# The delta-rule scan of a hybrid diffusion step: level products over all 128 rows of the TensorE array

## The reference

```
def step(S, inp):
    r_t, w_t, k_t, v_t, kk_t, a_t = inp
    sa = einsum('bdhvk,bdhk->bdhv', S, -kk_t)
    S = S * w_t[..., None, :] + sa[..., None] * (kk_t * a_t)[..., None, :] + v_t[..., None] * k_t[..., None, :]
    return S, einsum('bdhvk,bdhk->bdhv', S, r_t)
```

## Time and profile before

| what | value |
|---|---|
| median of 3 runs (lowest to highest) | 4503.6 us (4500.49 to 4511.37) |
| the profiled execution, its own time | 4488.36 us |
| its span | 4486.5 us |
| TensorE products busy, share of the span | 4088.9 us, 91% |
| VectorE busy | 2644.1 us, 59% |
| ScalarE busy | 1940.2 us, 43% |
| granted TensorE clock, mean over the span | 0.966 of full speed |

### The profile page before, as it was taken

How to read it: one execution, slowest core, us unless ns; L and a number is a source line. 1 busy time by engine, 2 the same in 40 slices (tenths; PEclk the granted TensorE clock), 3 DMA queues, 4 the chain that set the end, 5 groups by cost and what they waited for, 6 DMA issues and landing times. The chain is left out here.

```text
span 4486.5 us, 132472 instructions
## 1 busy us (share of the span) xinstructions
PE 4088.9 (91%) x58742; PEld 3518.4 (78%) x58742; DVE 2644.1 (59%) x4529; ACT 1940.2 (43%) x3640; POOL 92.4 (2%) x82
## 2 busy tenths in 40 slices
PE   6999978999988899899998999998999979999978
PEld 2888867888876799666668899886988868888858
DVE  6433557888866642455556433367524578888855
ACT  5333325666654531455554000045333256666642
POOL 0000000000110000000000000000000000001100
PEclk9999989999999899899999999999999989999989
DMA  8444765334434231100000222112345853334441
GB/s 314 145 127 134 221 206 147 101 104 103 99 68 158 79 70 41 53 1 1 2 15 24 98 95 71 43 62 69 114 124 174 255 163 107 103 107 100 92 151 59
DMA packets 541001, 470.96 MB, mean 105 GB/s; under 512 B 30096, under 2 KB 501264, under 8 KB 532752
## 3 DMA queue, kind: packets, MB, share of 16 engines
q1 hardware_dynamic: 389008, 386.96, 27.0%
q10 hardware_dynamic: 131840, 66.07, 5.1%
q0 software_dynamic: 19584, 9.44, 2.2%
HBM read 328.43 MB, written 128.71 MB: 102 GB/s over the span
## 5 line engine op out<-in xcount | busy, mean ns | idle before, releaser
L652 PE MATMUL ps<-big_r,stage_r 128*128 128x384 f32 x2976 | 638.8, 349 | 15.0 <-DVE big_r L914 13.6
L652 PEld LDWEIGHTS ps<-big_r,stage_r 128*128 128x128 f32 x2976 | 521.6, 189 | 69.2 <-issue 24.9
L2552 PE MATMUL ps<-big_r,w_out 128*128 128x384 f32 x2304 | 417.6, 341 | 36.1 <-DVE w_out L2668 35.8
L2552 PEld LDWEIGHTS ps<-big_r,w_out 128*128 128x128 f32 x2304 | 407.5, 191 | 44.6 <-DVE w_out L2668 38.8
L652 PE MATMUL ps<-big_r,w_slab_r 128*128 128x384 f32 x1488 | 340.6, 336 | 0.0
L369 PE MATMUL ps<-big_r,stage_r 128*128 128x384 f32 x1536 | 311.7, 337 | 13.2 <-DVE big_r L356 13.2
L2274 DVE TENSOR_REDUCE extra<-ps 128x1 f32<-128x1152 f32 (+1 forms) x144 | 177.7, 1234 | 204.0 <-PE ps L2179 204.0
L369 PEld LDWEIGHTS ps<-big_r,stage_r 128*128 128x128 f32 x1536 | 270.7, 189 | 27.8 <-issue 26.7
L1691 DVE COPY_PREDICATED arena<-arena,ps 128x128 f32<-128x128 uint32 x720 | 195.1, 328 | 123.6 <-PE ps L1305 121.1
L652 PEld LDWEIGHTS ps<-big_r,w_slab_r 128*128 128x128 f32 x1488 | 267.5, 189 | 0.0
L1513 ACT COPY arena<-ps 128x512 f32<-128x512 f32 x288 | 168.9, 586 | 205.1 <-PE ps L1319 204.9
(11 more groups left out here) (260 smaller groups left out, 8035.6 us busy)
## 6 DMA issues: line engine op xcount, KB each, us to landing
w_slab<-in_w SPq DMA_DIRECT2D x138, 512.0 KB, 3.3
arena<-scan_in SPq DMA_DIRECT2D x144, 320.0 KB, 3.7
arena<-scan_in SPq DMA_DIRECT2D x288, 128.0 KB, 3.7
scan_in<-x_resid ACTq DMA_DIRECT2D x48, 576.0 KB, 4.3
arena<-scan_in SPq DMA_DIRECT2D x48, 576.0 KB, 7.5
arena<-scan_in SPq DMA_DIRECT2D x144, 192.0 KB, 4.0
arena<-in_w_ada SPq DMA_DIRECT2D x24, 1024.0 KB, 5.9
x_resid<-in_w_ada SPq DMA_DIRECT2D x24, 1024.0 KB, 4.8
```

Source lines behind the costliest of these rows:

```text
L652: mm = pe.matmul(g.ps[:, 3 * s + c, 0:CW], w[:, k * P:(k + 1) * P], x[:, k, chunk(c)], start=k == i == 0, stop=k == NB - 1 and i == 2)
L2552: mm = pe.matmul(g.ps[:, bank(i, b), 0:wide[i]], w[:, b, k * P:(k + 1) * P], r, start=k == j == 0, stop=k == NB - 1 and j == 2)
```

## The change

The scan's levels k = 2 to 5 are made over all 128 rows of the array. A new buffer `xb` (in `g.slab`, which the scan didn't use) keeps the inverse so that the two chunks lie on rows 0 to 63 and 64 to 127 with zeros elsewhere, and `ba` (two buffers) keeps the gram blocks in the matching layout.

- `level_u` for k = 2 to 5 has 8 products of 128 rows by 64 columns with 64 moving columns, in place of 16 of 64 by 64 with 32. `level_x` for k = 2 to 4 has 8 of 128 by 64 with 64 in place of 16 of 64 by 64 with 64. Level 1 keeps its old products as `first_u` and `first_x`.
- `level_t` has 8 transposes of 64 rows by 128 columns (64 moving) in place of 4 of 128 by 128, and writes two PSUM banks, 1 and 2, in place of bank 2.
- `first_u(q)`, which writes banks 0 and 1, waits for `xt_ok` 5q - 1, that is for `copy_t(q - 1, 4)`.
- `copy_x` is two copies, each of 64 rows by 512 columns (k = 1) or 64 by 256 (k = 2 to 4), in place of one of 128 by 512. `level_t` and `level_u(q, 5)` wait for both.
- `copy_ba`, two copies of 64 by 512 from SBUF to SBUF per round, is new on ScalarE. `level_u(q, 2)` waits for both.
- `level_w` for k = 2 to 4 has two predicated copies of 64 by 256 in place of two of 128 by 128.
- GpSimd clears `xb` once at a scan's start. The constants for `w` get a layout to match.

```
@@ phase_scan: buffers
+    xb = g.slab[:, 0, 0:1024]
+    ba = [g.slab[:, 1, 512 * i:512 * i + 512] for i in range(2)]
...
@@ TensorE
-            def level_u(q, k):
-                n = 1 << k
-                if k == 1:
-                    pe.wait_ge(x_ok, q + 1)
-                    if q:
-                        pe.wait_ge(w_ok, 10 * q)
-                if k == 5:
-                    pe.wait_ge(xa_ok, 4 * q + 4)
+            def first_u(q):
+                n = 2
+                pe.wait_ge(x_ok, q + 1)
+                if q:
+                    pe.wait_ge(w_ok, 10 * q)
+                    pe.wait_ge(xt_ok, 5 * q - 1)
...
+            def level_u(q, k):
+                n = 1 << k
+                if k == 2:
+                    pe.wait_ge(ba_ok, 2 * q + 2)
+                if k == 5:
+                    pe.wait_ge(xa_ok, 8 * q + 8)
+                for d, s in U8:
+                    for h in range(2):
+                        u = 2 * d + s
+                        mm = pe.matmul(strided(ps, u * HD, (1, HD), rows=HALVES[h]),
+                                       strided(ba[q % 2], (4 * h + u) * HD, (1, HD)),
+                                       strided(xb, u * P + h * HD + d * n, (512, 2), (2 * n, 32 // n), (1, n)), start=True, stop=True)
+                mm.then_inc(u_mm, 1)
...
+            def level_x(q, k):
+                pe.wait_ge(w_ok, 10 * q + 2 * k)
+                pe.wait_ge(xt_ok, 5 * q + k - 1)
+                for d, s in U8:
+                    for p in range(2):
+                        u = 2 * d + s
+                        mm = pe.matmul(strided(ps, 512 + u * HD, (1, HD), rows=HALVES[p]),
+                                       strided(xt[q % 2], lx(d, p, s), (1, HD)),
+                                       strided(wk(k), (2 * u + p) * HD, (1, HD)), start=True, stop=True)
+                mm.then_inc(x_mm, 1)
...
             def level_t(q, k):
                 if k < 4:
-                    pe.wait_ge(xa_ok, 4 * q + k)
+                    pe.wait_ge(xa_ok, 8 * q + 2 * k)
...
-                    mm = pe.transpose(strided(ps, 2 * 512 + lx(d, 0, s), (P, 2), (1, HD)), strided(x, (2 * d + s) * P, (1, P)), g.ident[:, :])
+                    for p in range(2):
+                        u = 2 * d + s
+                        mm = pe.transpose(strided(ps, (1 + p) * 512 + u * HD, (1, HD)), strided(xb, p * 512 + u * P, (1, P), rows=HALVES[p]),
+                                          g.ident[HALVES[p], HALVES[p]])
...
@@ ScalarE
             def copy_x(q, k):
+                n = 1 << k
                 act.wait_ge(x_mm, 4 * q + k)
-                A.copy(strided(x, 0, (HD, 2), (P, 4), (1, HD)), strided(ps, 0, (512, 2), (HD, 4), (1, HD))).then_inc(xa_ok, 1)
+                for p in range(2):
+                    rows = HALVES[p]
+                    if k == 1:
...
+                        A.copy(strided(xb, p * 512, (HD, 2), (P, 4), (1, HD), rows=rows),
+                               strided(ps, 0, (512, 2), (HD, 4), (1, HD), rows=rows)).then_inc(xa_ok, 1)
+                    else:
+                        A.copy(strided(xb, p * 512, (256 + n, 2), (2 * n, P // n), (1, n), rows=rows),
+                               strided(ps, 512, (P, 2), (n, P // n), (1, n), rows=rows)).then_inc(xa_ok, 1)
+
+            def copy_ba(q, t):
+                act.wait_ge(g_ok, 4 * q + 2 * t + 2)
+                if q >= 2:
+                    act.wait_ge(u_mm, 5 * q - 5)
+                rows = HALVES[1 - t]
+                A.copy(strided(ba[q % 2], 0, (HD, 8), (1, HD), rows=rows),
+                       strided(gr[q % 3], t * 1024, (P, 8), (1, HD), rows=rows)).then_inc(ba_ok, 1)
...
                 if chain:
                     chain_sa(c, 1)
+                if nxt:
+                    copy_ba(q + 1, 0)
                 if here:
                     copy_x(q, 4)
...
                     copy_seeds(q + 1)
+                    copy_ba(q + 1, 1)
...
@@ VectorE, level_w
-                for p in range(2):
-                    V.copy_predicated(strided(wk(k), p * P, (256 + n, 2), (2 * n, HD // n), (1, n)),
...
+                for i in range(2):
+                    if k in (1, 5):
...
+                    else:
+                        V.copy_predicated(strided(wk(k), i * 32, (256, 2), (HD, 4), (1, 32), rows=HALVES[i]),
+                                          bits(strided(level_mask, (k - 1) * P, (HD, 2), (0, 4), (1, 32), rows=HALVES[i])),
+                                          strided(ps, 0, (P, 2), (32, 4), (1, 32), rows=HALVES[i])).then_inc(w_ok, 1)
...
@@ GpSimd
+            nc.gpsimd.memset(xb, 0.0).then_inc(blank_ok, 1)
             nc.gpsimd.memset(st_ctx, 0.0).then_inc(zero_ok, 1)

```

More of the change, by code:

```diff
@@ L1193, in phase_scan @@
             "tokv_ok", "rv_ok")
+        blank_ok, ba_ok = sem("blank_ok", "ba_ok")
         raw_in, y_st = [[sem(f"{n}{i}") for i in range(2)] for n in ("raw_in", "y_stored")]
@@ L1308, in level_u, with first_x @@
                 mm.then_inc(u_mm, 1)
[L1310 to L1315, removed]
+            def level_u(q, k):
[11 more added lines that the diff above has]
+                mm.then_inc(u_mm, 1)
+            def first_x(q):
+                pe.wait_ge(w_ok, 10 * q + 2)
+                pe.wait_ge(t1_ok, q + 1)
                 for d, s in U8:
@@ L1320, in level_x @@
                                            strided(xt[q % 2], lx(d, p, s), (1, HD), rows=HALVES[h]),
-                                           strided(wk(k), lx(d, p, s), (1, HD), rows=HALVES[h]), start=True, stop=True)
+                                           strided(wk(1), lx(d, p, s), (1, HD), rows=HALVES[h]), start=True, stop=True)
+                mm.then_inc(x_mm, 1)
[8 more added lines that the diff above has]
+                                       strided(wk(k), (2 * u + p) * HD, (1, HD)), start=True, stop=True)
                 mm.then_inc(x_mm, 1)
@@ L1435, in _ @@
                 if here:
-                    level_u(q, 1)
+                    first_u(q)
                     tokens_v(q)
@@ L1440, in _ @@
                 if here:
-                    level_x(q, 1)
+                    first_x(q)
                     tokens_bk(q)
@@ L1511, in copy_x @@
             def copy_x(q, k):
+                n = 1 << k
                 act.wait_ge(x_mm, 4 * q + k)
-                A.copy(strided(x, 0, (HD, 2), (P, 4), (1, HD)), strided(ps, 0, (512, 2), (HD, 4), (1, HD))).then_inc(xa_ok, 1)
+                for p in range(2):
+                    rows = HALVES[p]
+                    if k == 1:
+                        if q == p == 0:
+                            act.wait_ge(blank_ok, 1)
+                        A.copy(strided(xb, p * 512, (HD, 2), (P, 4), (1, HD), rows=rows),
[10 more added lines that the diff above has]
+                       strided(gr[q % 3], t * 1024, (P, 8), (1, HD), rows=rows)).then_inc(ba_ok, 1)
             def copy_seeds(q):
@@ L1541, in copy_t @@
                 if k < 5:
-                    A.copy(strided(xt[q % 2], n, (256 - n, 2), (2 * n, P // n), (1, n)),
-                           strided(ps, 2 * 512 + n, (256 - n, 2), (2 * n, P // n), (1, n))).then_inc(xt_ok, 1)
+                    A.copy(strided(xt[q % 2], n, (P, 2), (256 - n, 2), (2 * n, HD // n), (1, n)),
+                           strided(ps, 512 + n, (512, 2), (P - n, 2), (2 * n, HD // n), (1, n))).then_inc(xt_ok, 1)
                 else:
@@ L1689, in level_w @@
                     dve.wait_ge(t_mm, 5 * q)
-                for p in range(2):
-                    V.copy_predicated(strided(wk(k), p * P, (256 + n, 2), (2 * n, HD // n), (1, n)),
-                                      bits(strided(level_mask, (k - 1) * P, (HD, 2), (n, HD // n), (1, n))),
-                                      strided(ps, p * 512, (HD, 2), (n, HD // n), (1, n))).then_inc(w_ok, 1)
+                for i in range(2):
+                    if k in (1, 5):
+                        src = strided(ps, i * 512, (HD, 2), (n, HD // n), (1, n)) if k == 1 else strided(ps, i * 32, (P, 2), (HD, 2), (1, 32))
+                        V.copy_predicated(strided(wk(k), i * P, (256 + n, 2), (2 * n, HD // n), (1, n)),
+                                          bits(strided(level_mask, (k - 1) * P, (HD, 2), (n, HD // n), (1, n))), src).then_inc(w_ok, 1)
+                    else:
+                        V.copy_predicated(strided(wk(k), i * 32, (256, 2), (HD, 4), (1, 32), rows=HALVES[i]),
+                                          bits(strided(level_mask, (k - 1) * P, (HD, 2), (0, 4), (1, 32), rows=HALVES[i])),
+                                          strided(ps, 0, (P, 2), (32, 4), (1, 32), rows=HALVES[i])).then_inc(w_ok, 1)
             def copy_tokens(q):
@@ L2786, in constants @@
     levels = np.zeros((P, 5, 2, 2, 32), np.float32)
-    w = np.zeros((P, 5, 2, 2, 2, HD), np.float32)
+    w = np.zeros((P, 5, 512), np.float32)
+    head = np.arange(P)[:, None] // HD
     for k in range(1, 6):
@@ L2795, in constants @@
```

(6 more changed lines are left out.)

## The result

The changed kernel takes 4571.44 us (median of 3 runs, 4569.52 to 4572.73) against 4503.6 before: ratio 1.0145, 95% interval 1.0126 to 1.0165, 68 us slower. Forecast were 4643 us in a range of 4570 to 4725. The direction was right and the time lies just inside the range, but the rise is less than half of the 139 us that were forecast. The profiled execution is the one of 4571.44 us, span 4569.7; that of before was at 4488.36 under its median, so that between the two traces the spans differ by 83 us.

What follows compares the result with a forecast made beforehand. Rounds were taken as bound by TensorE's order. Smooth round +1.85, clock +0.43 and stalls -0.30 gave 1.98 us for 70 rounds, +139 us on 4503.6: 4643 us, range 4570 to 4725.

Steps and rivals of the forecast that it cites:

- What bounds the kernel, and that half the passes save nothing: Rounds bound by TensorE's order; half as many passes over twice the rows save nothing, 0.52 us against 0.48 for `level_u`.
- 64-row pace: Rival: new products run at the 64-row passes' 16 ns; round falls by 0.72 us, 4453 us in all; chance 0.03.
- weight loads no longer overlap: Rival: 16 new passes on TensorE take 3.2 us in place of 0.52, some 5960 us in all; chance 0.02.
- The new wait: `first_u` waits for ScalarE's `copy_t(q - 1, 4)`: 2.48 us after `turned_seeds`, not 0.98, so +1.50 us per round.
- The rest of the smooth round: Levels 1 to 4 up to `turned_seeds`, from changed products, transposes and copies: +0.35 us per round.
- The transposes: The 8 small transposes of `level_t` on TensorE: taken as 0.47 us, between 0.38 and 0.55.
- the predicated pair: VectorE's two copies of 64 by 256 in `level_w`: 0.76 us, where the pair took 0.50 before.
- the two halves of `copy_x(q, 1)`: ScalarE's level 1 copy: second half starts 0.48 us later and lasts 0.59, so `level_t(q, 1)` starts 0.31 later.
- The granted clock: TensorE's clock falls after the new idle time in a quarter of rounds, 1.7 us each: +0.43 us per round.
- The issue stalls: TensorE's idle stretches put down to "issue": -0.3 us of 1.2 us per round, ends 0 and -1.2.
- the misread row: The second scan's first `seeds`, taken at 3632.42 us; it gave a mean round of 18.66 us, 1.2 over the smooth one.
- The stalls vanish: Rival: the new wait takes in all issue stalls, leaving 0.65 us per round, +46 us, 4549 us; chance 0.11.

Runs made afterwards that it cites:

- The first experiment: Kernel before, with only one edit: a round's first `level_u` waits for `copy_t(q - 1, 4)`, without any new copy; 4542.83 us, ratio 1.0117.
- the third: Changed kernel with `copy_ba(q + 1, 1)` moved behind `copy_t(q, 4)` on ScalarE; 4510.56 us, ratio 1.0038 to the kernel before.

## Why the prediction was wrong in size, and right in part

*What bounds the kernel, and that half the passes save nothing:* right. Sixteen passes of the new form take 0.52 us, as `chain_state` did. The rivals "64-row pace" and "weight loads no longer overlap" are out by the same row: the new products start 0.0325 us apart and last 0.69 - 15 x 0.0325 = 0.20, so they overlap. This is against the rule of the Trainium skill ("TensorE: Matmul & The Clock Gate", Part 3) as it stands there, since all of them use every row group.

*The new wait, +1.50 us:* right; 2.54 - 0.98 = 1.56. The first experiment alone gives its part without the copy, 0.97 forecast and 0.97 measured; the third that of the copy, 0.53 forecast and 0.51 measured.

*The rest of the smooth round, +0.35:* near; +0.45. The transposes were cheaper (0.39 from start to start against 0.47), the predicated pair (0.92 against 0.76) and the two halves of `copy_x(q, 1)` (1.19 against 1.07) dearer. With the wait met early the smooth round shows this part by itself: 17.90 - 17.45 = 0.45.

*The granted clock, +0.43:* near: 20 of 70 rounds (a quarter forecast) at 1.5 us (1.7 forecast) are 0.43 us a round, but before already had some 0.1 of it (five falls behind the scans' starts), so that it rose by some 0.3.

*The issue stalls, -0.30:* **this is the term that was mis-sized.** The stretches over the smooth round that aren't falls of the clock shrank from 1.45, less some 0.1 for the few falls of before, to 0.51 - 0.43 = 0.08: -1.3 us a round. That is more than the end of -1.2 that was given, which rested on the misread row. The 1.0 us too little here, less 0.06 by which the other terms together came out higher, is the difference between the 1.98 us a round that were forecast and the 1.07 that came, 64 us in 70 rounds. The rest of the way to the two medians is no term of the sum: 8 us came from outside the rounds, and the trace of before lies 15 us under its median. "The stalls vanish" was held to be a rival that needs the new wait to absorb them, with 0.11; they vanished together with everything else that was forecast, and for another cause. The wait does absorb some (1.45 to 1.19), but with the new form and no idle wait they are gone as well (0.26 and 0.20). The prediction did name the 96 passes fewer beside the stalls, but worked nothing out from them: -0.3 is a choice between its ends of 0 and -1.2. It found that the new form saves no time on TensorE, and did not ask what the same time with half the instructions does to stalls that are late instructions.

That the stalls are TensorE's instructions arriving late is shown by the packets. That long runs of short passes at the fast pace bring them on is argued from the kernels as a whole: it fits all nine, and the 3.26 us between packets, but why one packet comes late and the next does not was not followed up.

## What to carry to other kernels

A wait that is added because a buffer is now shared costs what its signal has queued in front of it on the other engine. Before adding it, move the releasing instruction to the earliest place where its input is ready; here one moved copy turns 1.5% slower into 1.2% faster. And when products are recast into half as many of twice the rows, price the stalls that TensorE has with nothing to wait for, here its late instructions, and not the busy time alone: compare a mean round with a smooth one, and count all rounds before dividing.

## What was not expected of the hardware

The same idle 1.42 us per round was followed by 20 falls of the clock in the changed kernel, with its products of 128 rows, but by few in the kernel with the old products and the same waiting (9 in both scans, starts and stalls included). With 0.91 us there were 4 falls in the kernel with `copy_ba` last and 7 with the wait alone, starts included, and before had 7. What else decides is open.

The idle stretches that the profile puts down to "issue" were late blocks of TensorE's instructions, in every case that these traces have. Three times 32 passes put back into a round brought few of them when a piece lasted 1.12 us (0.30 us over the smooth round), half of them when it lasted 0.67 (0.74), and 96 in one piece brought all of them (1.41).
